# Seven products in place of eight for the last two slabs of the second mixer's input projection

## The chip, the cores and the metric

The kernel runs on one core of one Trainium2 chip, in fp32 throughout. The metric is the device time of one execution in microseconds (us), as the median of several runs. PE is TensorE (matmuls), PEld its weight loads, DVE VectorE, ACT ScalarE, POOL GpSimd, SP SyncE, which issues nearly all DMAs here. SBUF is the on-chip memory, PSUM the eight banks into which matmuls write. "L875" is line 875 of the kernel before.

## What is computed

Two layers over 256 tokens of width 1024, each a mixer (attention) and then a mixture of experts, with residual adds. The change lies in the input projection of the second layer's mixer:

```python
def _mixer_c(h, w_in, qn, kn, w_out):
    proj = jnp.einsum('bsd,de->bse', h, w_in)        # 1024 -> 1536 columns
    q, k, v = jnp.split(proj, C_SPLITS, axis=-1)     # 16 query heads, 4 key and value heads of 64
    q = _rmsnorm(q.reshape(b, S, C_HEADS, HEAD_DIM), qn)
    k = _rmsnorm(k.reshape(b, S, C_KV_HEADS, HEAD_DIM), kn)
    q = _apply_axial_rope(q, cr, sr, cc, sc)
    k = _apply_axial_rope(k, cr, sr, cc, sc)
    o = _dense_blocked_attention(q, k, v).reshape(b, S, C_QW)
    return jnp.einsum('bse,ed->bsd', o, w_out)
```

Behind it follow the output projection, the residual, the router and 32 experts, each a SwiGLU MLP of width 256, all of whose weights are read from HBM (96 MB per layer).

## The kernel before

**Weights.** All weights stream through slots of 1 MB in SBUF: 19 slots of `ring` (0 to 18), four of `shared`, one in `xT` and one in `heads` at the times when these are free. The units are numbered in the order of use: layer 0 has 9 slabs of the input projection (0 to 8), 4 output units and 96 expert units, layer 1 has slabs 109 to 114, output units 115 to 118 and expert units from 119 on. `place_units` fixes for each unit its slot and whose use it waits for; SP issues the loads in this order (L743, or L747 where several units go together), and waits in front of each until its slot is free (`s_used`, counted by PE). A load whose slot is not free holds back all behind it.

**Slabs.** A slab is 256 columns of the projection: 8 chunks of 128 rows by two halves of the tokens, 16 matmuls 128x128x256 into one PSUM bank (L875; `open_slab` at L850 for slab 0). The profile counts two records for each fp32 matmul of the source, so a slab is 32 records. `parts(s, 0, 1, 2, 3)` are its quarters. In layer 1, slab 0 holds the keys, slab 1 the values, slabs 2 to 5 four query heads each. Behind a slab of queries or keys, ACT copies it to `unturned` and squares it (L1316, L1317), DVE makes the inverse root (`norm`, L1673 to L1699) and the rotation (`rotate`, L1712 to L1729 or L1736), PE transposes it (`turn`, L957, L954) and ACT copies it to `heads` (L1380).

**Attention** goes by pairs of heads: `scores` on PE (L977), `maxima` on DVE (L1746), exponentials on ACT (L1394), `normalise` on DVE (L1773, L1776), `turn_prob` on PE (L994) with a copy on ACT (L1409), `prob_values` on PE (L1005) with a copy on ACT (L1413). Pairs 0 and 1 need slab 2, pairs 2 and 3 slab 3, pairs 4 and 5 slab 4, pairs 6 and 7 slab 5. `rows((cp, k))` is one piece of the output projection (L1017): quarter cp of the output, head pair k; it adds to a bank that already holds the residual (`residual(cp)`, ACT, L1432).

**Seven products.** Layer 0 treats six of its slabs in three pairs (`PAIRED`) by Strassen's scheme in Winograd's form. A pair of slabs is seen as a 2x2 block product (token halves by halves of the contraction, halves of the contraction by the two slabs): seven products of 4 matmuls, 8 records each (L891), instead of eight. It needs four sums of the input (`tokens`, L1616, once), four of the weights (`weights`, L1630, per pair, one of them written over a slab's weights), and five sums of products on DVE (`add_product`, L1638 to L1657) with three copies on ACT. Product order is 1, 5, 6, 7, 2, 3, 4. The slab named second is complete after product 3, the first after product 4. The sums lie in ring slots 15 to 17.

**Order.** One list per layer, `ORDER_0` and `ORDER_1`, is written out by hand. Each engine goes through the same list and issues its own part of each entry, and then works strictly in this order; waits are on semaphores. In layer 1, before:

```python
            + each("norm", 1) + each("rotate", 2) + parts(3, 0, 1, 2, 3) + parts(4, 0) + each("turn", 2) + parts(4, 1)
            + each("norm", 2) + attend(0) + parts(4, 2, 3) + each("residual", 0) + each("rotate", 3)
            + each("normalise", 0) + parts(5, 0) + each("norm", 3)
            + each("turn_prob", 0) + attend(1) + each("turn", 3) + parts(5, 1)
            + each("prob_values", 0) + each("normalise", 1) + parts(5, 2)
            + each("turn_prob", 1) + each("rotate", 4) + attend(2) + parts(5, 3) + each("residual", 1)
            + each("prob_values", 1) + each("normalise", 2) + rows((0, 0))
            + each("turn_prob", 2) + attend(3) + each("turn", 4) + rows((0, 1), (1, 0))
```

`norm` counts groups: group 0 is slab 0, groups 1 to 4 are slabs 2 to 5; `rotate` and `turn` count slabs.

## Time and profile before

| | us |
|---|---|
| median of 3 runs | 615.95 (615.41 to 616.2) |
| profiled execution | 618.22, span in the trace 616.1 |
| PE busy | 563.8 (92%) |
| DVE busy | 207.0 (34%) |
| ACT busy | 136.0 (22%) |
| HBM read | 231.60 MB, 378 GB/s over the span |

The span is the time from the first to the last event of the trace; the device time of the same execution is 2.1 us longer. Layer 1 begins at about 318 us in the trace, its experts at about 430 us. A busy share is a mean over stages with different limits: what counts is which wait ends last in the stage of the change. Tables by stage, timelines of single engines and the chain that ended last are read for that.

### The profile page before, as it was taken

How to read it: one execution, taken by the hardware profiler on the slowest of the kernel's cores; microseconds unless marked ns; L12 is line 12 of the kernel's file. 1: busy time of each engine (PE TensorE's matmuls, PEld its weight loads, DVE VectorE, ACT ScalarE, POOL GpSimd, SP SyncE). 2: the span in 40 equal slices, each digit the busy share in tenths (PEclk: the TensorE clock that was granted, in tenths of full speed). 3: DMA queues.
4: the chain of work that ended last, by engine and by line, in shares of the span. 5: the costliest groups of instructions: out<-in, count | busy, mean ns of one | idle time of the engine just before them, and what ended most of it. 6: DMA issues, size and time to landing. Idle time of an engine off the chain costs nothing.

```text
span 616.1 us, 9586 instructions
## 1 busy us (share of the span) xinstructions
PE 563.8 (92%) x3876; PEld 373.2 (61%) x3876; DVE 207.0 (34%) x631; ACT 136.0 (22%) x354; POOL 8.6 (1%) x25
## 2 busy tenths in 40 slices
PE   7999999998999949998999999999899996997997
PEld 6887877883555333555468876779355535434454
DVE  3778766153111101111035687416211111011101
ACT  2134547241001101001031366524100110110101
POOL 1100000000000000000011000000000000000000
PEclk8999999999999969999999999999999997999899
DMA  8992899789999999999999994539999999999996
GB/s 319 423 422 73 321 423 420 272 316 429 424 426 439 433 415 439 425 429 414 421 415 421 421 419 191 205 135 341 391 424 427 428 438 428 427 431 433 412 420 262
DMA packets 24229, 233.39 MB, mean 379 GB/s; under 512 B 2672, under 2 KB 3312, under 8 KB 6640
## 3 DMA queue, kind: packets, MB, share of 16 engines
q1 hardware_dynamic: 22448, 228.19, 88.8%
q10 hardware_dynamic: 1728, 4.47, 2.0%
q8 instruction: 36, 0.59, 0.4%
q14 instruction: 17, 0.14, 0.1%
HBM read 231.60 MB, written 1.05 MB: 378 GB/s over the span
## 4 chain that ended last, share of the span: by engine, by line
PE 58%; DMA 20%; issue 4%; ACT 3%; DVE 2%; DVEq 0%
DMA ring<-in_moe_w 20%; PE banks L1151 13%; PE banks L1017 8%; PE banks L1125 7%; PE banks L875 6%; PE banks L1221 6%; PE banks L1237 5%; PE banks L977 2%; PE banks L1005 1%; PE banks L994 1%; PE banks L1136 1%; PE banks L1028 1%; PE banks L1053 1%; PE banks L850 1%; PE banks L1094 1%
## 5 line engine op out<-in xcount | busy, mean ns | idle before, releaser
L1151 PE MATMUL banks<-ring,desk 128*32 128x512 f32 x736 | 86.4, 608 | 6.3 <-DMA ring<-in_moe_w 6.2
L1497 ACT ACTIVATE desk<-banks 128x256 f32<-128x256 f32 x16 | 6.1, 384 | 272.8 <-PE banks L1151 272.8
L1125 PE MATMUL banks<-desk,hT 128*128 128x128 f32 x384 | 49.9, 293 | 14.2 <-issue 14.2
L1017 PE MATMUL banks<-heads,ring 128*128 128x256 f32 x256 | 61.7, 386 | 0.1
L1125 PEld LDWEIGHTS banks<-desk,hT 128*128 128x128 f32 x384 | 49.4, 209 | 15.5 <-issue 15.0
L1151 PEld LDWEIGHTS banks<-ring,desk 128*32 128x32 f32 x736 | 22.8, 112 | 55.8 <-issue 50.8
L1017 PEld LDWEIGHTS banks<-heads,ring 128*128 128x128 f32 x256 | 46.4, 190 | 11.9 <-issue 6.2
L1221 PE MATMUL banks<-ring,desk 128*32 128x512 f32 x400 | 46.2, 595 | 8.1 <-ACT desk L1499 6.2
L1237 PE MATMUL banks<-desk 128*128 128x256 f32 x224 | 52.1, 386 | 0.0
L1237 PEld LDWEIGHTS banks<-desk 128*128 128x128 f32 x224 | 41.4, 190 | 16.8 <-issue 11.7
L875 PE MATMUL banks<-ring,hT 128*128 128x256 f32 x224 | 50.3, 381 | 0.0
L1913 DVE TENSOR_TENSOR desk<-banks,desk 128x256 f32<-128x256 f32 x16 | 6.8, 425 | 121.7 <-ACT desk L1497 121.7
L875 PEld LDWEIGHTS banks<-ring,hT 128*128 128x128 f32 x224 | 41.8, 190 | 6.4 <-issue 1.0
L1878 DVE TENSOR_TENSOR desk<-banks,gains_xT 128x512 f32<-128x512 f32 x24 | 16.6, 692 | 82.8 <-PE banks L1125 82.8
L1919 DVE COPY desk<-banks 128x512 f32<-128x512 f32 x14 | 9.7, 691 | 67.9 <-PE banks L1221 67.9
L1221 PEld LDWEIGHTS banks<-ring,desk 128*32 128x32 f32 x400 | 11.8, 109 | 32.7 <-issue 23.5
L891 PE MATMUL banks<-ring 128*128 128x256 f32 x96 | 22.9, 385 | 0.0
L891 PEld LDWEIGHTS banks<-ring 128*128 128x128 f32 x96 | 17.6, 190 | 3.9 <-issue 1.8
L850 PE MATMUL banks<-ring,hT 128*128 128x256 f32 x64 | 16.7, 423 | 2.0 <-DVE hT L1592 2.0
L1187 PE MATMUL banks<-small,desk 128*128 128x128 f32 x32 | 6.9, 297 | 12.4 <-DVE desk L1913 12.4
L977 PE MATMUL banks<-shared,heads 64*128 64x256 f32 x128 | 18.1, 402 | 0.1
L1151 PE MATMUL banks<-ring,heads 128*32 128x512 f32 x128 | 16.2, 601 | 1.9 <-DMA ring<-in_moe_w 1.9
(205 smaller groups left out, 654.0 us busy)
## 6 DMA issues: line engine op xcount, KB each, us to landing
ring<-in_moe_w SPq DMA_DIRECT2D x66, 1024.0 KB, 26.5
ring<-in_moe_w SPq DMA_DIRECT2D x16, 4096.0 KB, 26.8
ring<-in_moe_w SPq DMA_DIRECT2D x17, 2048.0 KB, 12.3
ring<-in_ab_w_in SPq DMA_DIRECT2D x8, 1024.0 KB, 17.0
shared<-in_moe_w SPq DMA_DIRECT2D x8, 1024.0 KB, 7.5
shared<-in_moe_w SPq DMA_DIRECT2D x2, 4096.0 KB, 30.9
shared<-in_moe_w SPq DMA_DIRECT2D x3, 2048.0 KB, 16.2
ring<-in_c_w_in SPq DMA_DIRECT2D x5, 1024.0 KB, 20.6
```

Source lines behind the costliest of these rows:

```text
L850: ins = pe.matmul(bank2(SLAB_BANK[layer][0], NT)[:, t, :], hT[:, c, t * P:(t + 1) * P], slab_weights(layer, 0)[:, c, :], start=(c == 0 and ...
L875: ins = pe.matmul(bank2(SLAB_BANK[layer][s], NT)[:, t, :], hT[:, c, t * P:(t + 1) * P], w[:, c, :], start=(c == 0 and t == 0), stop=(c == ...
L891: ins = pe.matmul(out, a[:, c, :], b[:, c, :], start=(start and c == 0), stop=(c == NC // 2 - 1), skip_group_check=True)
L977: ins = pe.matmul(bank2(r, NT)[:, t, :], heads[rows, i, t * P:(t + 1) * P], keysT[rows, kt, :], start=(t == 0), stop=True, skip_group_chec ...
L1017: ins = pe.matmul(bank2(Y[cp], 2)[:, c % 2, :], w[:, k % 2, c * P:(c + 1) * P], attT[:, k, :], start=False, stop=(k == PAIRS - 1 and c % 2 ...
L1125: ins = pe.matmul(bank(2 + half)[:, c * P:(c + 1) * P], tokens[:, t, half * HALF + c * P:half * HALF + (c + 1) * P], onehot_of(rd, to)[:, ...
L1151: ins = pe.matmul(bank(0)[j * SLOTS:(j + 1) * SLOTS, :], gathered_of(rd, place)[:, c, j * SLOTS:(j + 1) * SLOTS], w[:, j, :], start=(c == ...
L1187: pe.transpose(bank(4)[:, k * P:(k + 1) * P], hidden[:, k * P:(k + 1) * P], ident)
L1221: ins = pe.matmul(bank(2 + half)[j * SLOTS:(j + 1) * SLOTS, :], hiddenT[:, k, j * SLOTS:(j + 1) * SLOTS], w, start=(k == 0), stop=(k == 1))
L1237: ins = pe.matmul(bank2(Y[c // 2], 2)[:, c % 2, :], outputs[:, c * P:(c + 1) * P], scatter, start=False, stop=(c % 2 == 1), skip_group_che ...
L1878: V.tensor_tensor(gathered_of(rd, place)[:, 4 * h:4 * h + 4, :], bank2(2 + h, 4), gains[:, 2 * rd.layer + 1, 4 * h:4 * h + 4].unsqueeze(2) ...
L1919: V.tensor_copy(outputs[:, HALF:D], bank(3)).then_inc(sig.out_v, 1)
```

## The change

Slabs 5 and 4 of layer 1 become a fourth pair in `PAIRED` (first 5, second 4), with the banks 6 and 7 (slabs 4 and 5 exchange their banks) and half of bank 5, the bank of `turn`, for product 4. The sums of the tokens are made again from the second layer's input, in the same place. In `place_units` the slots 15 to 17 take no unit of layer 1 until both slabs of the pair are used; DVE waits in front of the first sums until the last units of layer 0 in these slots are used (`SUMS_FREE`). `ORDER_1` gets the token sums at its head, the weight sums behind the rotation of slab 0, the seven products in place of the eight quarters of slabs 4 and 5, and some entries change places: the norm of slab 4 goes behind product 4, `residual` 0 and 1 and the output rows (0,0) and (1,0) are moved. Helper functions get the layer or the pair as an argument. The core of the diff:

```diff
-PAIRED = ((3, 4), (5, 6), (8, 7))
+PAIRED = ((3, 4), (5, 6), (8, 7), (5, 4))
+IN_FIRST = 3
 SUMS_AT = 15
+SUM_SLOTS = 3
...
+        if layer:
+            last = first_unit(1, "in") + max(PAIRED[IN_FIRST])
+            left = [free[s] for s in range(SUMS_AT, SUMS_AT + SUM_SLOTS)]
+            for s in range(SUMS_AT, SUMS_AT + SUM_SLOTS):
+                free[s] = (last, last)
...
-        SLAB_BANK = [[6, 7, 2, 7, 6, 6, 7, 6, 7], [2, 3, 6, 7, 6, 7]]
+        SLAB_BANK = [[6, 7, 2, 7, 6, 6, 7, 6, 7], [2, 3, 6, 7, 7, 6]]
...
         ORDER_1 = (
-            each("sums", 0) + each("rstd", 0) + each("norm", 0) + each("rotate", 0) + parts(1, 0, 1, 2, 3)
+            each("tokens", 1) + each("sums", 0) + each("rstd", 0) + each("norm", 0) + each("rotate", 0)
+            + sums(3, 3, 1, 2, 4) + parts(1, 0, 1, 2, 3)
             + each("values", 1) + parts(2, 0, 1) + each("turn", 0) + parts(2, 2) + [("turn", 0, 1)] + parts(2, 3)
-            + each("norm", 1) + each("rotate", 2) + parts(3, 0, 1, 2, 3) + parts(4, 0) + each("turn", 2) + parts(4, 1)
-            + each("norm", 2) + attend(0) + parts(4, 2, 3) + each("residual", 0) + each("rotate", 3)
-            + each("normalise", 0) + parts(5, 0) + each("norm", 3)
-            + each("turn_prob", 0) + attend(1) + each("turn", 3) + parts(5, 1)
-            + each("prob_values", 0) + each("normalise", 1) + parts(5, 2)
-            + each("turn_prob", 1) + each("rotate", 4) + attend(2) + parts(5, 3) + each("residual", 1)
-            + each("prob_values", 1) + each("normalise", 2) + rows((0, 0))
-            + each("turn_prob", 2) + attend(3) + each("turn", 4) + rows((0, 1), (1, 0))
+            + each("norm", 1) + each("rotate", 2) + parts(3, 0, 1, 2, 3) + products(3, 1) + each("turn", 2) + products(3, 5)
+            + each("norm", 2) + attend(0) + products(3, 6) + each("rotate", 3) + products(3, 7)
+            + each("normalise", 0) + products(3, 2)
+            + each("turn_prob", 0) + attend(1) + each("turn", 3) + each("residual", 0) + products(3, 3)
+            + each("prob_values", 0) + each("normalise", 1) + products(3, 4) + each("norm", 3)
+            + each("turn_prob", 1) + each("residual", 1) + each("rotate", 4) + attend(2) + rows((0, 0))
+            + each("prob_values", 1) + each("normalise", 2) + rows((1, 0))
+            + each("turn_prob", 2) + attend(3) + each("turn", 4) + rows((0, 1))
...
-            return bank2(0, NT)[:, 1, :] if pair == len(PAIRED) - 1 else pair_banks(pair)[0][:, 1, :]
+            spare = {IN_FIRST - 1: 0, IN_FIRST: 5}
+            return bank2(spare[pair], NT)[:, 1, :] if pair in spare else pair_banks(pair)[0][:, 1, :]
...
                 if j == 1:
-                    if pair:
+                    if layer:
+                        slab_taken(pe, 1, 2)
+                    elif pair:
                         pe.wait_ge(s_tiles, 3 * pair - 1)
                     else:
                         slab_taken(pe, 0, 1)
-                    slab_arrived(0, first)
+                    slab_arrived(layer, first)
                     multiply(x[:, 0, :], hT[:, low_half, rows_0], wa[:, low_half, :], start=True).then_inc(s_prod, 1)
                 elif j == 5:
-                    if pair:
+                    if layer:
+                        slab_taken(pe, 1, 3)
+                    elif pair:
                         pe.wait_ge(s_tiles, 3 * pair)
                     else:
                         slab_taken(pe, 0, 0)
-                    pe.wait_ge(s_tsum, 1)
+                    pe.wait_ge(s_tsum, 4 * layer + 1)
                     pe.wait_ge(s_wsum, 4 * pair + 2)
                     multiply(y[:, 0, :], token_sum[:, 0, :, :], wb[:, low_half, :], start=True).then_inc(s_prod, 1)
...
                     pe.wait_ge(s_wsum, 4 * pair + 4)
                     pe.wait_ge(s_c11, pair + 1)
-                    if pair == len(PAIRED) - 1:
+                    if layer:
+                        pe.wait_ge(s_hT, turns_before(1, second))
+                    elif pair == IN_FIRST - 1:
                         pe.wait_ge(s_sc, NT * A_HEADS)
                     multiply(fourth_of(pair), hT[:, high_half, rows_1], t4, start=True).then_inc(s_used, 2)
...
+                    if layer and s == PAIRED[IN_FIRST][1]:
+                        pe.wait_ge(s_tiles, 3 * len(PAIRED))
...
-                if layer == 0 and cp == 0:
-                    act.wait_ge(s_tiles, 3 * len(PAIRED) - 1)
-                elif layer == 0 and cp == 1:
-                    act.wait_ge(s_c11, len(PAIRED))
+                if cp < 2 and cp == layer:
+                    act.wait_ge(s_tiles, 3 * (IN_FIRST + layer) - 1)
                 elif cp < 2:
-                    slab_taken(act, layer, max(s for s in range(SLABS[layer]) if SLAB_BANK[layer][s] == Y[cp]))
+                    act.wait_ge(s_c11, IN_FIRST + layer)
                 elif cp == 2:
...
-            def add_tokens():
+            def add_tokens(layer):
                 a11, a21 = hT[:, 0:NC // 2, 0:P], hT[:, 0:NC // 2, P:SEQ]
                 a12, a22 = hT[:, NC // 2:NC, 0:P], hT[:, NC // 2:NC, P:SEQ]
                 s1, s2, s3, s4 = [token_sum[:, i, :, :] for i in range(4)]
-                dve.wait_ge(s_h, 4)
+                dve.wait_ge(s_h, 4 * (layer + 1))
+                if layer:
+                    dve.wait_ge(s_used, SUMS_FREE)
                 for i, (out, a, b, op) in enumerate(((s1, a21, a22, ALU.add), (s2, s1, a11, ALU.subtract),
                                                      (s3, a11, a21, ALU.subtract), (s4, a12, s2, ALU.subtract))):
-                    after(dve, s_tsum, i)
+                    after(dve, s_tsum, 4 * layer + i)
                     V.tensor_tensor(out, a, b, op).then_inc(s_tsum, 1)
...
                 if i == 3:
                     for s in PAIRED[pair]:
-                        unit_arrived(dve, s)
-                    if pair >= 2:
+                        unit_arrived(dve, at + s)
+                    if pair >= IN_FIRST:
+                        dve.wait_ge(s_used, SUMS_FREE)
+                    elif pair >= 2:
                         pair_done(dve, pair - 2)
                 else:
                     dve.wait_ge(s_wsum, 4 * pair + (3, 1, 2, 4).index(i))
...
+            def buffer_turned(pair, s):
+
+                if pair >= IN_FIRST:
+                    dve.wait_ge(s_slab, norm_slabs_before(1, s) - 1)
+                elif SLAB_PLAN[0][s][0] in ("heads", "keys"):
                     dve.wait_ge(s_hT_ps, turns_before(*NORMED[norm_slabs_before(0, s) - 1]))
```

On ACT, `take_product` copies product 1 to `kept`, product 5 to `fifth` and product 2 to the first slab's tile, and squares each finished slab, as in layer 0.

## Rows read from the trace of the kernel before

**Rows 1.** The page's slices: 40 of 15.4 us; granted clock in tenths, GB/s moved.

```profile
...
PEclk8999999999999969999999999999999997999899
...
GB/s 319 423 422 73 321 423 420 272 316 429 424 426 439 433 415 439 425 429 414 421 415 421 421 419 191 205 135 341 391 424 427 428 438 428 427 431 433 412 420 262
...
```

**Rows 2.** Table by stage: busy us (instructions) by engine, granted clock, DMA share, GB/s.

```profile
...
375.00:388.00 13.00, 12.69 (x82) 8.36 (x80) 11.24 (x38) 7.91 (x27) 0.00 (x0) 1.00 0.24 81
435.00:607.00 172.00, 150.93 (x1171) 82.30 (x1168) 25.14 (x51) 12.91 (x32) 0.00 (x0) 0.96 1.00 427
512.00:514.00 2.00, 0.00 (x0) 0.00 (x0) 0.00 (x0) 0.00 (x0) 0.00 (x0) 1.00 1.11 455
514.00:515.00 1.00, 0.00 (x0) 0.00 (x0) 0.00 (x0) 0.00 (x0) 0.00 (x0) 0.50 0.84 360
...
```

**Rows 3.** Timeline of SyncE's DMA issues: start, us, line, operation.

```profile
...
304.16 7.43 SPq L743 DMA_DIRECT2D ring<-in_c_w_in  x4
...
431.30 3.35 SPq L743 DMA_DIRECT2D ring<-in_moe_w  x3
...
```

**Rows 4.** The chain that ended last, in order of time: start, us, what.

```profile
...
338.94 10.36 PE banks L875 x48
...
379.85 0.69 DVE negmax L1746
...
389.30 1.13 PE banks L1017 x4
...
```

**Rows 5.** Timeline of PE: start, us, line, tiles, records, [idle before it].

```profile
...
286.27 3.64 PE L1221 MATMUL banks<-ring,desk 128*32 128x512 f32 x32 [1.90 <-DMA ring<-in_moe_w]
...
371.85 1.13 PE L977 MATMUL banks<-shared,heads 64*128 64x256 f32 x8
...
383.41 0.66 PE L994 MATMUL banks<-small,shared 128*128 128x128 f32 x4 [0.26 <-DVE shared L1776]
...
515.87 6.16 PE L1125 MATMUL banks<-desk,hT 128*128 128x128 f32 x32 [5.12 <-issue]
...
```

**Rows 6.** Timeline of DVE in layer 1, columns the same.

```profile
...
325.91 0.16 DVE L1570 TENSOR_SCALAR mean<-banks 128x2 f32<-128x2 f32 x1 [2.78 <-PE banks L860]
...
333.26 1.80 DVE L1736 TENSOR_TENSOR desk<-desk 128x256 f32<-128x256 f32 x4
341.83 0.69 DVE L1673 TENSOR_REDUCE head_ss<-shared 128x8 f32<-128x512 f32 x1 [6.76 <-ACT shared L1317]
...
352.64 1.29 DVE L1746 TENSOR_REDUCE negmax<-banks 128x2 f32<-128x512 f32 x2 [0.47 <-PE banks L977]
...
357.50 0.68 DVE L1673 TENSOR_REDUCE head_ss<-shared 128x8 f32<-128x512 f32 x1
...
360.84 1.28 DVE L1746 TENSOR_REDUCE negmax<-banks 128x2 f32<-128x512 f32 x2
...
364.25 0.42 DVE L1712 TENSOR_TENSOR desk<-shared 128x256 f32<-128x256 f32 x1
...
367.15 1.29 DVE L1746 TENSOR_REDUCE negmax<-banks 128x2 f32<-128x512 f32 x2 [0.60 <-PE banks L977]
...
373.08 1.29 DVE L1746 TENSOR_REDUCE negmax<-banks 128x2 f32<-128x512 f32 x2 [2.43 <-PE banks L977]
...
```

**Rows 7.** The page's costliest groups: busy us, mean ns, idle before.

```profile
...
L875 PE MATMUL banks<-ring,hT 128*128 128x256 f32 x224 | 50.3, 381 | 0.0
...
L891 PE MATMUL banks<-ring 128*128 128x256 f32 x96 | 22.9, 385 | 0.0
...
```

**Rows 8.** Timeline of DVE in layer 0: sums of tokens, weights and products.

```profile
...
19.32 0.69 DVE L1616 TENSOR_TENSOR ring<-hT 128x512 f32<-128x512 f32 x1
...
28.40 5.00 DVE L1630 TENSOR_TENSOR ring<-ring 128x1024 f32<-128x1024 f32 x4
...
71.29 0.42 DVE L1638 TENSOR_TENSOR shared<-shared,banks 128x256 f32<-128x256 f32 x1 [0.46 <-PE banks L891]
...
```

**Rows 9.** The last four slab loads of layer 1, from issue to landing.

```profile
...
DMA to landing us min/median/max: 20.0/20.5/21.1
```

More of the change, by code:

```diff
@@ L154, in place_units @@
 def place_units():
-    last = max(PAIRED[-1])
+    last = max(PAIRED[IN_FIRST - 1])
     free = {s: (-1, None) if s < SUMS_AT else (last, last) for s in range(LOW)}
@@ L192, in place_units @@
             (high if s >= LOW else free)[s] = (seen, n)
-    return where
-WHERE = place_units()
+    return where, max(int(n) for n, _ in left) + 1
+WHERE, SUMS_FREE = place_units()
 def hybrid_moe_kernel(nc, xT_d, small_d, bias_d, rope_d, ab_in, ab_out, c_in, c_out, experts_d, out_d):
@@ L882, in product @@
                 first, second = PAIRED[pair]
+                layer = layer_of(pair)
                 x, y = pair_banks(pair)
-                wa, wb = slab_weights(0, first), slab_weights(0, second)
-                t2, t3, t4 = [weight_sums[:, pair % 2, i, :, :] for i in range(3)]
+                wa, wb = slab_weights(layer, first), slab_weights(layer, second)
+                t2, t3, t4 = [weight_sums[:, sums_region(pair), i, :, :] for i in range(3)]
                 low_half, high_half = slice(0, NC // 2), slice(NC // 2, NC)
@@ L923, in product @@
                     pe.wait_ge(s_v, pair + 1)
-                    pe.wait_ge(s_tsum, 4)
-                    slab_arrived(0, second)
+                    pe.wait_ge(s_tsum, 4 * layer + 4)
+                    slab_arrived(layer, second)
                     multiply(y[:, 0, :], token_sum[:, 3, :, :], wb[:, high_half, :]).then_inc(s_prod, 1)
@@ L1318, in slab, with room_for @@
                              ACT.Square).then_inc(s_sqh, 1)
[L1320 to L1322 removed]
+            def room_for(layer, s):
+                i = norm_slabs_before(layer, s)
                 act.wait_ge(s_slab, i - 1)
[L1324 removed]
+                if layer == 0:
+                    act.wait_ge(s_hT_ps, turns_before(*NORMED[i - 1]))
             def take_product(pair, j):
                 first, second = PAIRED[pair]
+                layer = layer_of(pair)
                 x, y = pair_banks(pair)
@@ L1336, in take_product @@
                     product_done(act, pair, 2)
-                    kind, _, col, _ = SLAB_PLAN[0][first]
+                    kind, _, col, _ = SLAB_PLAN[layer][first]
                     if kind == "values":
@@ L1342, in take_product @@
                     if kind != "shared2":
-                        room_for(first)
-                    A.activation(tile_of(first, 0), x[:, 0, :], ACT.Copy).then_inc(s_c11, 1)
+                        room_for(layer, first)
+                    A.activation(tile_of(pair, first, 0), x[:, 0, :], ACT.Copy).then_inc(s_c11, 1)
                 elif j in (3, 4):
@@ L1641, in add_product @@
                     dve.wait_ge(s_u, pair + 1)
-                    if pair and SLAB_PLAN[0][PAIRED[pair - 1][0]][0] == "values":
+                    if 0 < pair < IN_FIRST and SLAB_PLAN[0][PAIRED[pair - 1][0]][0] == "values":
                         dve.wait_ge(s_val, values_before(0, PAIRED[pair - 1][0]) + 1)
                     V.tensor_tensor(widened, kept, y[:, 1, :], ALU.add).then_inc(s_v, 1)
-                    buffer_turned(second)
+                    buffer_turned(pair, second)
                     dve.wait_ge(s_p5, pair + 1)
                     dve.wait_ge(s_v, pair + 1)
-                    V.tensor_tensor(tile_of(second, 1), widened, fifth, ALU.add).then_inc(s_tiles, 1)
+                    V.tensor_tensor(tile_of(pair, second, 1), widened, fifth, ALU.add).then_inc(s_tiles, 1)
                 elif j == 3:
@@ L1651, in add_product @@
                     dve.wait_ge(s_tiles, 3 * pair + 1)
-                    V.tensor_tensor(tile_of(second, 0), kept, y[:, 0, :], ALU.add).then_inc(s_tiles, 1)
+                    V.tensor_tensor(tile_of(pair, second, 0), kept, y[:, 0, :], ALU.add).then_inc(s_tiles, 1)
                 elif j == 4:
@@ L1965, in _ @@
                     elif what == "tokens":
-                        add_tokens()
+                        add_tokens(layer)
                     elif what == "weights":
```

41 lines of the change are left out of this document (21 added, 20 removed).

## The prediction

> **What bounds the kernel now.** I read the page's slices first. The two layers look alike: a mixer, then experts. In the experts the DMA engines move 410 to 440 GB/s without a break; in the second mixer they fall to 191, 205 and 135 GB/s [rows 1]. The table by stage says the same: from 435 us to 607 us the DMA share is 1.00, from 375 to 388 us it is 0.24, with TensorE (PE) busy for 12.69 of the 13 us [rows 2]. So the tail is bound by transfers, and the time at which it may begin is set by PE in the second mixer: the ring is full, and SyncE waits for slots. The load that ends the last standstill is the three expert units issued from 431.30 us [rows 3], when the first expert unit of layer 1 has been used. By my reading of the planner, units 0 to 143 are under way at that point both before and after, so whatever the mixer takes more or less reaches the end one for one.
>
> What bounds the mixer itself is told by the chain of waits. Up to 371.85 us it is PE's own work. Then it leaves PE: maxima of pair 3 on VectorE (DVE) at 373.08, maxima of pair 4 at 379.85, maxima of pair 5, ScalarE's (ACT) residual copy, and only at 389.30 PE again, with the row (2,0) [rows 4, 5, 6]. Between 373.08 and 389.30 lie 16.2 us of DVE and ACT work with no slack. Before it DVE has some: it waited 2.43 us for PE at 373.08 and 0.60 at 367.15 [rows 6]. This is where the change works.
>
> **The change part by part.** A source matmul is two records, one record 0.216 us (10.36 us for 48) [rows 4].
>
> Products for slabs: slabs 4 and 5 are 64 records, seven products of 8 are 56. Removed 13.8 us, added 12.1: PE is 1.7 us shorter. Product records of layer 0 have the duration of slab records (385 against 381 ns) [rows 7].
>
> Token sums: four DVE operations of 0.69 us, 0.73 apart [rows 8], 2.9 us. They stand where DVE waits 2.78 us for PE before 325.91. The rotation of slab 0 ends at 333.26 + 1.80 = 335.06, PE wants it at 336.2, so up to 1.1 us more would be hidden [rows 6]. Cost 0; without that cover 2.9.
>
> Weight sums: four of 1.22 us, 5.0 together [rows 8]; from 335.06 they end at 340.1, inside the 6.76 us in which DVE waits for slab 2 (until 341.83) [rows 6]. Cost 0. They wait for slabs 4 and 5: the issues of the last four slabs end at 311.6, landing takes 21.1 us at most, so 332.7 against 335.06 [rows 3, 9]. If slab 5 came late, slab 2's norm, queued behind, would wait; 1.7 us of that is free.
>
> Three ring slots kept until product 4: five expert loads (units 129 to 133) wait for it and issue near 366 us. DMA may pause for some 4 us before it, but the pause comes out of the standstill that starts at 375 us anyway [rows 2], since the next loads wait for the last slab's rotation. Cost 0, and nothing in the mixer needs them.
>
> "Fifth slab rotated in front of the third pair's maxima": rotation of slab 4 at 364.25, maxima 2 at 367.15 [rows 6]: it stood in front before, too. What moves is the norm of slab 4. Before, slab 4 was complete early and its norm ran at 357.50, between normalise 0 and maxima 1 (360.84: 3.34 us) [rows 6]. Now it is ready only after product 3, and the list puts norm and rotation behind product 4's sum. That is the step on which I place the forecast, so the queues in turn, from the end of slab 3 at 347.4:
>
> PE: product 1 to 349.2, turn 2 to 349.6, product 5 to 351.3, scores 0 to 352.4, products 6, 7, 2 to 357.6. DVE: maxima 0 at 352.64 as before. From there to the end of normalise 0 it needed 4.86 us (to 357.50) [rows 6]; inserted are the sum after product 6 (waits until 354.2, 0.4 of idle) and two after product 7, each 0.35 to 0.42 as in layer 0 [rows 8], 1.2 us. Normalise 0 ends at 359.1 and turn_prob 0 is over at 359.6 where PE could have been at 358.5: **1.1 us of the 1.7 are lost here**.
>
> PE on: scores 1 360.6, turn 3 361.1, product 3 362.9, values 0 363.9, product 4 365.6, turn_prob 1 366.5, scores 2 367.6, row (0,0), values 1, row (1,0) to 370.3. DVE: maxima 1, sum of product 3 (to 363.3), normalise 1 (to 364.8), sum of product 4 (waits, to 366.1), norm of slab 4 + 3.34 = 369.4, rotation + 2.2 = 371.6, **maxima 2 at 371.6, before 367.15** [rows 6]. PE has nothing left that it may do: turn_prob 2 needs normalise 2. Where DVE set the pace (pair 4), the second head's transposes began 3.56 us after the maxima (379.85 to 383.41), and they take 0.6 until the next scores, 4.15 in all [rows 4, 5]. Pair 2's so end at 375.75, and scores 3 start there, before at 371.85 [rows 5]: +3.9.
>
> Scale of the sum: the same durations put end to end give before's own third scores 0.5 us too early by the view, half of it taken up by the waits on DVE: +0.2, so I take +4.0 (rounded down). From scores 3 on the DVE chain of 16.2 us is the same in both, and it has no slack to give back. Row (1,0), pulled ahead, fills PE but is not on that chain. Mixer: **+4.0 us**.
>
> On the other queues: ACT gets three copies and two squares of 0.4 to 0.6 us instead of two slabs' copies and squares; its product 4 squares stand in front of turn_prob 1's copies, but product 4's sum (366.1) precedes those transposes' end anyway. Cost 0.
>
> Bounds: if the 1.1 us at turn_prob 0 is not lost (sums hidden), +2.9. If every sum costs 0.42 and each hand-over 0.1 more, +4.6. The profiled run took 618.22 (span 616.1 and 2.1 around it), the median is 615.95; the shift is added to both: 622.2 profiled, **620.0 as median**.
>
> **The rivals.** (a) *PE's idle time halves its clock.* In the gap of about 3.9 us ahead of turn_prob 2 PE does nothing. The trace shows a gap of 5.12 us before 515.87, in which the granted clock is 1.00 until 514 us and then falls to 0.50 (1.2 GHz); the 32 records behind it take 6.16 us [rows 2, 5]; the one of 1.90 before 286.27 left it high [rows 1, 5]. 3.9 lies between. If it falls, half a turn_prob (0.5) and scores 3 (1.06) are paid twice on the chain: +1.5, giving 621.5. For: nearer to 5.12 than to 1.9. Against: the clock was still 1.00 for over 3 us of that gap. The Trainium skill, "TensorE: Matmul & The Clock Gate", section "HAM oscillation — how this bites in real kernels", warns against such idle gaps in PE, each paid with a cold start; by it this case would be the likelier, by the rows it may just escape.
>
> (b) *PE's saving arrives: faster.* Place: turn_prob 2. If normalise 2 is ready when PE has done row (1,0), PE goes on 1.7 us early (0.7 with the loss at turn_prob 0), and the chain from scores 3 starts earlier by as much: 614.3 to 615.3. For this maxima 2 has to start by 367.8, so norm 3 by 362.2, before product 3 is even out (362.9). For it speaks only that PE is the busier engine in the mixer (12.69 of 13 us busy against DVE's 11.24 [rows 2]); against it the order of DVE's queue.
>
> (c) *The shift is partly absorbed behind the mixer*: the row at 389.30 had slack I don't see, or loads pace the rows. 617 to 618.5. Behind 389.30 the chain goes on with PE's own work and no wait up to the experts, so little speaks for it.
>
> (d) *The change does not do what it says*, the rotation being in front already: in itself 0, and contained in the forecast.
>
> **How the numbers follow.** Forecast (+2.9 to +4.6) 0.56, (a) 0.20, (b) 0.10, (c) 0.14, of which 0.08 within the bound. About 0.2% (1.2 us) is what a measurement of this kernel can tell from no change. Slower by more: 0.56 + 0.20 + 0.06 = 0.82; within 0.08; faster 0.10. The range reaches from 618.0 (upper part of (c)) to 622.0 (above (a) with 0.5 of spread) and leaves out (b) and the rest of (c).
>
> **What would show it.** Right: in the profile after, maxima 2 near 371.6 to 372, an idle time of PE of 3 to 4 us in front of turn_prob 2, scores 3 near 375.8, DVE without gaps from about 366 to 376, the row (2,0) near 393.3, and the load behind the first expert unit at 435.3. The sums of tokens and weights should lie in what were gaps, with turn 0 still at 336.2. Clock: 0.50 in 374 to 380 would be (a). Wrong: maxima 2 before 368; or maxima 2 late and the load of 431.3 not late; or a wait of the weight sums for slab 5, which would show as a late norm of slab 2 after 341.83.

## The result: 622.47 us, where 615.68 was measured before

Timed beside the kernel before, the changed kernel takes **622.47 us** (median of 6 runs, 621.93 to 624.28) against 615.68 us (614.81 to 616.2): ratio 1.0116, interval 1.0100 to 1.0131. It is slower by 6.8 us. The forecast was 620.0 us with a range from 618.0 to 622.0, so the direction is right and the size is not. The changed program was timed twice more, each time beside new runs of before, and was slower by 5.7 and 6.4 us there.

The page of the changed kernel, to set beside [rows 1]: the span, busy time of PE and DVE, granted clock in tenths of full speed and GB/s in 40 slices of 15.5 us.

```profile
span 620.2 us, 9596 instructions
...
PE 565.3 (91%) x3868; PEld 373.9 (60%) x3868; DVE 216.2 (35%) x644; ACT 136.2 (22%) x355; POOL 11.5 (2%) x25
...
PEclk9999999999999969999999997999999997999899
...
GB/s 325 423 422 59 388 420 424 268 314 435 424 425 444 415 435 433 427 431 412 417 418 420 422 296 192 203 93 377 352 430 426 438 428 428 434 424 431 416 421 262
```

The slices with little DMA in the second mixer now read 192, 203 and 93 GB/s where they read 191, 205 and 135. Slices of 15 us are coarse and lie differently against the two mixers; by how much the loads come later is told by their issue times below. The experts behind run at the same rate.

**A clock for the mixer.** Spans alone mislead here: in the profiled execution of before, layer 0 happens to be about 2 us longer than in most others (layer 1 begins at 318.46 us there, at 318.28 in e2 and at 315.8 to 316.8 in all others). So I count the mixer from its own start, the first slab's 32 records, to the issue of the three expert units behind which the tail begins. The start, in the timeline of PE of the kernel before, and then start and end in those of PE and of SP's queue of the changed kernel:

```profile
...
318.46 7.07 PE L850 MATMUL banks<-ring,hT 128*128 128x256 f32 x32
...
```

```profile
...
316.46 7.07 PE L866 MATMUL banks<-ring,hT 128*128 128x256 f32 x32
...
```

```profile
...
435.60 3.34 SPq L759 DMA_DIRECT2D ring<-in_moe_w  x3
...
```

That is 119.14 us, and before it was 431.30 [rows 3] less 318.46 = 112.84: the mixer is **6.30 us longer**. From that load to the end it is 184.6 us, before 184.8. The tail hands the shift on one for one. Times of the changed kernel called "aligned" below have 2.00 us added.

DVE in layer 1, to set beside [rows 6] (start, us, line, tiles, count, [idle before it, and what ended it]):

```profile
...
323.28 0.69 DVE L1643 TENSOR_TENSOR ring<-hT,ring 128x512 f32<-128x512 f32 x1
323.90 0.16 DVE L1595 TENSOR_SCALAR mean<-banks 128x2 f32<-128x2 f32 x1
...
333.02 5.00 DVE L1660 TENSOR_TENSOR ring<-ring 128x1024 f32<-128x1024 f32 x4
...
339.82 0.69 DVE L1705 TENSOR_REDUCE head_ss<-shared 128x8 f32<-128x512 f32 x1 [1.80 <-ACT shared L1342]
...
350.63 1.29 DVE L1778 TENSOR_REDUCE negmax<-banks 128x2 f32<-128x512 f32 x2 [0.47 <-PE banks L1002]
352.49 0.42 DVE L1668 TENSOR_TENSOR shared<-shared,banks 128x256 f32<-128x256 f32 x1 [0.57 <-PE banks L908]
...
355.03 0.41 DVE L1674 TENSOR_TENSOR shared<-shared,banks 128x256 f32<-128x256 f32 x1
355.58 0.42 DVE L1678 TENSOR_TENSOR shared<-shared 128x256 f32<-128x256 f32 x1
...
359.33 1.29 DVE L1778 TENSOR_REDUCE negmax<-banks 128x2 f32<-128x512 f32 x2 [1.88 <-PE banks L1002]
...
364.63 0.42 DVE L1687 TENSOR_TENSOR shared<-shared,banks 128x256 f32<-128x256 f32 x1 [1.17 <-PE banks L908]
364.96 0.68 DVE L1705 TENSOR_REDUCE head_ss<-shared 128x8 f32<-128x512 f32 x1
...
370.63 1.28 DVE L1778 TENSOR_REDUCE negmax<-banks 128x2 f32<-128x512 f32 x2
...
377.41 1.29 DVE L1778 TENSOR_REDUCE negmax<-banks 128x2 f32<-128x512 f32 x2 [3.28 <-PE banks L1002]
...
```

L1778 is the maxima. Those of pair 2 start at 370.63, aligned 372.63, where before had 367.15. They stand behind norm and rotation of slab 4 (from 364.96), and the norm stands behind product 4's sum (364.63), though the slab it needs was complete after product 3. Those of pair 3 start at 377.41, aligned 379.41, where before had 373.08: +6.33, the whole of the mixer's loss. The maxima of pair 4 follow 6.76 us later (384.17), in before 6.77.

PE around the place, beside [rows 5]:

```profile
...
356.88 1.29 PE L1019 MATMUL banks<-small,shared 128*128 128x128 f32 x8 [0.97 <-DVE shared L1808]
...
368.53 1.13 PE L1042 MATMUL banks<-heads,ring 128*128 128x256 f32 x4
373.27 2.03 PE L1019 MATMUL banks<-small,shared 128*128 128x128 f32 x8 [3.60 <-DVE shared L1808]
375.23 2.08 PE L1002 MATMUL banks<-shared,heads 64*128 64x256 f32 x8
...
```

PE idles 3.60 us in front of turn_prob 2 (L1019), and the scores behind it (L1002) take 2.08 us, where the third scores of before took 1.13 [rows 5]. The table by stage says why (stretch, length, busy time of PE, PEld, DVE, ACT and POOL, granted clock, DMA share, GB/s):

```profile
...
370.00:372.00 2.00, 0.00 (x0) 0.00 (x0) 1.89 (x3) 0.66 (x3) 0.00 (x0) 1.00 0.97 369
372.00:373.00 1.00, 0.00 (x0) 0.00 (x0) 0.57 (x3) 1.00 (x5) 0.00 (x0) 0.64 1.00 418
373.00:374.00 1.00, 0.73 (x4) 0.71 (x4) 0.87 (x4) 0.55 (x3) 0.00 (x0) 0.50 1.08 451
374.00:376.00 2.00, 2.00 (x10) 1.40 (x10) 0.13 (x1) 1.20 (x2) 0.00 (x0) 0.50 0.97 410
...
378.00:379.00 1.00, 1.00 (x4) 0.82 (x3) 0.70 (x2) 0.87 (x4) 0.00 (x0) 0.50 0.87 369
379.00:380.00 1.00, 1.00 (x7) 0.58 (x7) 0.78 (x3) 1.00 (x7) 0.00 (x0) 0.95 0.20 82
...
```

The granted clock falls to 0.50 (1.2 GHz) within the gap and stays there until about 379 us: rival (a) has come true.

### The profile page after: what moved, and what is told of

It is laid out like the page before. It is cut to its first block, busy times and chain, and to the rows that moved or that the text cites. A ratio compares the mean times of both kernels' runs of the same rounds, so it can differ in the third digit from the quotient of the medians.

```text
span 620.2 us, 9596 instructions
## 1 busy us (share of the span) xinstructions
PE 565.3 (91%) x3868; PEld 373.9 (60%) x3868; DVE 216.2 (35%) x644; ACT 136.2 (22%) x355; POOL 11.5 (2%) x25
## 3 DMA queue, kind: packets, MB, share of 16 engines
HBM read 231.60 MB, written 1.05 MB: 375 GB/s over the span
## 4 chain that ended last, share of the span: by engine, by line
PE 58%; DMA 19%; issue 4%; DVE 4%; ACT 3%; DVEq 0%
DMA ring<-in_moe_w 19%; PE banks L1176 13%; PE banks L1042 8%; PE banks L1150 7%; PE banks L1246 6%; PE banks L1262 6%; PE banks L891 3%; PE banks L1002 2%; PE banks L1019 2%; PE banks L908 1%; PE banks L1030 1%; PE banks L1161 1%; PE banks L1053 1%; PE banks L1078 1%; PE banks L866 1%
## 5 line engine op out<-in xcount | busy, mean ns | idle before, releaser
L891 PE MATMUL banks<-ring,hT 128*128 128x256 f32 x160 | 35.4, 380 | 0.0
L891 PEld LDWEIGHTS banks<-ring,hT 128*128 128x128 f32 x160 | 30.1, 190 | 3.9
L908 PE MATMUL banks<-ring 128*128 128x256 f32 x128 | 30.4, 384 | 0.0
L908 PEld LDWEIGHTS banks<-ring 128*128 128x128 f32 x128 | 23.4, 190 | 4.9 <-issue 2.1
L908 PE MATMUL banks<-ring,hT 128*128 128x256 f32 x96 | 22.7, 383 | 0.1
L908 PEld LDWEIGHTS banks<-ring,hT 128*128 128x128 f32 x96 | 17.7, 190 | 3.7 <-issue 1.5
L1660 DVE TENSOR_TENSOR ring<-ring 128x1024 f32<-128x1024 f32 x16 | 19.6, 1223 | 0.3
L1002 PE MATMUL banks<-shared,heads 64*128 64x256 f32 x128 | 19.1, 419 | 0.1
```

The source lines that it names most:

```text
L891: ins = pe.matmul(bank2(SLAB_BANK[layer][s], NT)[:, t, :], hT[:, c, t * P:(t + 1) * P], w[:, c, :], start=(c == 0 and t == 0), stop=(c == ...
L908: ins = pe.matmul(out, a[:, c, :], b[:, c, :], start=(start and c == 0), stop=(c == NC // 2 - 1), skip_group_check=True)
L1002: ins = pe.matmul(bank2(r, NT)[:, t, :], heads[rows, i, t * P:(t + 1) * P], keysT[rows, kt, :], start=(t == 0), stop=True, skip_group_chec ...
L1660: V.tensor_tensor(out, a, b, ALU.subtract).then_inc(s_wsum, 1)
```

## The experiments

All are read by the mixer's length, taken as above. Medians and ratios are those of several runs beside before; the other columns are of one profiled execution. PE busy is over the mixer's interval.

| kernel | median us | ratio (interval) | mixer us | against before | PE busy us |
|---|---|---|---|---|---|
| before | 615.68 to 616.13 | | 112.84 | | 112.39 |
| changed | 622.47 | 1.0116 (1.0100 to 1.0131) | 119.14 | +6.30 | 114.09 |
| e7, the same again | 621.67 | 1.0091 (1.0077 to 1.0105) | 118.81 | +5.97 | |
| e10, the same again | 622.10 | 1.0112 (1.0095 to 1.0129) | 118.86 | +6.02 | |
| e1, PE kept busy | 621.72 | 1.0092 (1.0067 to 1.0117) | 117.76 | +4.92 | |
| e9, the same again | 621.07 | 1.0083 (1.0069 to 1.0097) | 117.76 | +4.92 | 114.67 |
| e11, half as busy | 622.03 | 1.0101 (1.0085 to 1.0116) | 119.17 | +6.33 | |
| e2, norm late in before | 617.38 | 1.0018 (1.0008 to 1.0027) | 114.17 | +1.33 | |
| e3, sums without products | 615.78 | 0.9993 (0.9982 to 1.0005) | 112.85 | +0.01 | |
| e6, two entries moved | 618.90 | 1.0044 (1.0031 to 1.0058) | 115.81 | +2.97 | |
| e4, products, other order | 613.98 | 0.9969 (0.9958 to 0.9981) | 110.79 | -2.05 | 110.16 |
| e8, the same again | 613.95 | 0.9962 (0.9948 to 0.9976) | 110.79 | -2.05 | |
| e5, before, other order | 614.51 | 0.9978 (0.9968 to 0.9988) | 111.50 | -1.34 | 111.50 |

The tail from the load to the end is 184.5 to 184.9 us in all of them.

**PE kept busy in the gap (e1, e9).** In `turn_prob` of the changed kernel, 14 matmuls whose results nobody reads fill most of the gap (0.49 us of it is left):

```diff
+                if layer and i == 2:
+                    pe.wait_ge(s_pT, HEADS + 2 * i)
+                    warm_up(2, ident, 14)
```

> The changed kernel, with 14 matmuls of the identity by itself (128x128x128 each, 0.22 us each, some 3.1 us in all, into a bank that is overwritten next) in front of turn_prob of pair 2 in the second mixer, where PE stands idle for 3.60 us. Their results are not used. Theory 'queue and clock': of the 6.3 us by which the maxima of pair 3 come late against the kernel before, 1.4 us are the halved clock behind the gap (the transposes of turn_prob 2 take 2.03 us in place of 1.04, scores 3 take 2.08 in place of 1.13). With PE busy in the gap the granted clock stays at 1.00, maxima 3 begin about 5.4 us behind maxima 2 in place of 6.78, and the time falls by 1.4 us: about +5.4 us against the kernel before (621.1). Rival 'the chain does not care': PE's slow stretch is covered by DVE's and ACT's work, then the clock stays up and the time stays within 0.3 us of the changed kernel.

> The changed kernel with 14 identity matmuls in PE's gap, once more, now beside the changed kernel on the same chip, since the first run was told by few executions. Theory 'the halved clock costs on the chain': 1.0 to 1.4 us below the changed kernel. Rival 'the clock costs nothing in the end': equal to it within 0.3 us.

The timeline of PE in e1, and three stretches of its table:

```profile
...
369.41 3.29 PE L1056 MATMUL banks<-small 128*128 128x128 f32 x28
373.19 0.66 PE L1022 MATMUL banks<-small,shared 128*128 128x128 f32 x4 [0.49 <-DVE shared L1811]
374.10 0.66 PE L1022 MATMUL banks<-small,shared 128*128 128x128 f32 x4 [0.26 <-DVE shared L1811]
374.69 1.13 PE L1002 MATMUL banks<-shared,heads 64*128 64x256 f32 x8
...
```

```profile
...
372.00:373.00 1.00, 0.70 (x7) 0.51 (x5) 0.65 (x3) 1.00 (x6) 0.00 (x0) 1.00 1.04 442
373.00:374.00 1.00, 0.66 (x4) 0.42 (x4) 0.87 (x4) 0.59 (x4) 0.00 (x0) 1.00 0.99 418
374.00:376.00 2.00, 1.90 (x14) 1.36 (x15) 0.13 (x2) 1.08 (x2) 0.00 (x0) 1.00 1.01 426
...
```

With work in the gap the clock stays at 1.00 (2.4 GHz), the scores take 1.13 us again, and from the maxima of pair 2 to those of pair 3 it is 5.38 us (370.54 to 375.92) instead of 6.78. The mixer is 1.38 us shorter, in both traces. In device time it is 1.0 us (621.07 for e9 against 622.10 for e10, measured side by side); the ratios' intervals (1.0069 to 1.0097, 1.0095 to 1.0129) touch, so the trace carries this more firmly than the medians. What is left at full clock, +4.92, is not the clock's; e2, e3, e6 and e4 below show how much of it is the order's.

**The changed kernel again (e7, e10).** The same program, measured beside the others on their chip.

> The changed kernel itself, beside the others on the same chip: 6.3 to 6.8 us above the kernel before. It shows whether the halved clock behind the gap is there in another profile (the transposes of turn_prob 2 at 2.0 us, scores 3 at 2.1 us).

> The changed kernel, for the comparison with the kernel above and the one below: 5.7 to 6.8 us above the kernel before, the halved clock behind the gap in front of turn_prob 2 again.

Its excess over before scatters (5.7, 6.4, 6.8 us; e7 came out under the 6.3 to 6.8 that I expected), and the traces give a reason for some of it: the moment at which the clock falls is not the same. In e10, PE and the table by stage:

```profile
...
372.61 0.66 PE L1019 MATMUL banks<-small,shared 128*128 128x128 f32 x4 [3.62 <-DVE shared L1808]
373.52 0.79 PE L1019 MATMUL banks<-small,shared 128*128 128x128 f32 x4 [0.26 <-DVE shared L1808]
374.24 2.08 PE L1002 MATMUL banks<-shared,heads 64*128 64x256 f32 x8
...
```

```profile
...
372.00:374.00 2.00, 1.13 (x8) 0.84 (x8) 1.34 (x5) 1.49 (x6) 0.00 (x0) 0.98 1.05 438
374.00:376.00 2.00, 2.00 (x10) 1.19 (x8) 0.00 (x0) 0.60 (x1) 0.00 (x0) 0.50 0.97 410
376.00:378.00 2.00, 2.00 (x10) 1.57 (x8) 1.29 (x2) 0.86 (x4) 0.00 (x0) 0.67 1.07 451
...
```

The idle time is the same (3.62 us), but the clock falls only just before 374, when the transposes are nearly done: they cost 0.13 more than at full clock instead of 0.45, the scores 0.95 in both. So the same gap costs 1.10 us here (118.86 less 117.76) and 1.38 in the first trace. e7 is like e10: the two heads' transposes take 0.65 and 0.77 us, not the 2.0 in all that I expected, and the scores 2.08.

**Half as much filler (e11).** The edit of e1 with 6 matmuls instead of 14.

> The changed kernel with 6 identity matmuls (1.3 us) at the start of the same gap of 3.6 us, so that PE is idle for about 2.3 us in front of turn_prob 2. In the traces so far stalls of 1.46 and 1.90 us left the granted clock at 1.00, those of 3.60 us let it fall. If the fall takes a gap of nearly the full length, the clock stays up and the time is that of the 14 matmuls; if any idle time over some 2 us is enough, it falls to 0.50 and the time is that of the changed kernel.

```profile
...
369.43 1.50 PE L1056 MATMUL banks<-small 128*128 128x128 f32 x12
373.21 0.66 PE L1022 MATMUL banks<-small,shared 128*128 128x128 f32 x4 [2.28 <-DVE shared L1811]
374.12 1.12 PE L1022 MATMUL banks<-small,shared 128*128 128x128 f32 x4 [0.25 <-DVE shared L1811]
375.16 2.08 PE L1002 MATMUL banks<-shared,heads 64*128 64x256 f32 x8
...
```

```profile
...
373.00:374.00 1.00, 0.66 (x4) 0.42 (x4) 0.87 (x4) 0.59 (x4) 0.00 (x0) 0.95 0.99 418
374.00:376.00 2.00, 1.88 (x8) 1.47 (x10) 0.06 (x1) 1.10 (x2) 0.00 (x0) 0.50 1.02 430
...
```

The filler leaves 2.28 us of idle time, and the clock falls all the same, just before 374 us, when PE is at work again; the second head's transposes take 1.12 us instead of 0.66, the scores 2.08. The mixer takes 119.17 us, as in the first trace of the changed kernel (119.14), and 0.3 more than in e10 beside it. A filler that covers the gap in part buys nothing here.

That a gap of this length is enough doesn't hang on the filler. In layer 0 of e6, PE had worked without a break for 14 us (257.71 to 272.14), and then stood idle for 2.56 us:

```profile
...
274.70 5.34 PE L1176 MATMUL banks<-ring,desk 128*32 128x512 f32 x32 [2.56 <-DMA ring<-in_moe_w]
...
```

The granted clock reads 1.00 up to 275 us, 0.55 over 275 to 276 and 0.50 over 276 to 278, and the 32 records take 5.34 us. After an idle time of 2.38 us at the same place in e11 they take 5.34 too; after 1.97 us in e8, 3.64 us at a clock of 1.00.

**The norm of slab 4 late, without any product (e2).** In before's list:

```diff
-            + each("normalise", 0) + parts(5, 0) + each("norm", 3)
+            + each("normalise", 0) + parts(5, 0)
...
-            + each("prob_values", 0) + each("normalise", 1) + parts(5, 2)
+            + each("prob_values", 0) + each("normalise", 1) + parts(5, 2) + each("norm", 3)
```

> The kernel before (plain slabs, no sums, no products) with one entry moved: the norm of slab 4 stands where the changed kernel has it, behind normalise 1 in place of behind normalise 0. Theory 'order of the DVE queue': norm and rotation of slab 4 (5.5 us) now stand together in front of the maxima of pair 2. Norm of slab 4 starts near 364.2 in place of 357.5, maxima 2 near 369.5 in place of 367.15, turn_prob 2 waits, and the mixer ends later by about 1.2 us (617.0 against 615.7). That is only a part of the changed kernel's delay, since here the norm can start 2.7 us earlier than behind product 4. Rival 'it is the sums and products themselves, not their order': no change within 0.3 us.

PE at turn_prob 2, in the kernel before and in e2:

```profile
...
370.88 1.04 PE L994 MATMUL banks<-small,shared 128*128 128x128 f32 x8
...
```

```profile
...
371.50 0.65 PE L994 MATMUL banks<-small,shared 128*128 128x128 f32 x4 [0.65 <-DVE shared L1776]
...
```

The maxima of pair 2 start 1.9 us later (50.58 us after the mixer's start instead of 48.69) and PE now waits 0.65 us for `normalise` in front of turn_prob 2, where before shows no wait. The mixer grows by 1.33 us and the median by 1.25. So the move of the norm alone, with every matmul as it was, makes the kernel slower, through the queue of DVE.

**The sums without the products (e3).** The changed kernel's slots, token sums and weight sums, with before's slabs, banks and order of slabs behind them; sum 1 goes to another region, so that slab 4's weights stay whole, and PE waits for all eight sums in front of slab 4.

```diff
+                    if layer and s == 4:
+                        pe.wait_ge(s_wsum, 4 * len(PAIRED))
+                        pe.wait_ge(s_tsum, 8)
```

> The changed kernel's sums without its products: token sums, weight sums and the three ring slots kept for them as in the changed kernel, but slabs 4 and 5 as eight quarters in the order of the kernel before, on the banks of before. The sums are not used. (One weight sum goes to the sums' own place, not over slab 4's weights; PE waits in front of slab 4 for sums that have long been made.) Theory 'queue and clock': the sums lie in idle time of DVE, the slots in a standstill of the loads, so the time is that of the kernel before within 0.3 us (615.7). Rival 'the sums or the slots cost': 0.5 to 3 us more, seen as a late turn of slab 0 or a late load behind the first expert unit.

The mixer takes 112.85 us against 112.84, and the ratio's interval holds 1. Eight DVE operations of 7.9 us in all, three slots held back and the wait for slabs 4 and 5 cost nothing: they lie in idle time.

**Two entries moved (e6).** In the changed kernel, the norm of slab 4 goes in front of product 4, as early as its data allows, and its rotation behind the maxima of pair 2. The second goes beyond the kernel before, where the rotation stood in front of these maxima too.

```diff
-            + each("prob_values", 0) + each("normalise", 1) + products(3, 4) + each("norm", 3)
-            + each("turn_prob", 1) + each("residual", 1) + each("rotate", 4) + attend(2) + rows((0, 0))
+            + each("prob_values", 0) + each("normalise", 1) + each("norm", 3) + products(3, 4)
+            + each("turn_prob", 1) + each("residual", 1) + attend(2) + each("rotate", 4) + rows((0, 0))
```

> The changed kernel with two entries moved in DVE's queue and nothing else: the norm of slab 4 in front of product 4's sum (it needs only product 3's), the rotation of slab 4 behind the maxima of pair 2. By the sum of durations maxima 2 start 3.0 us earlier, the idle time of PE in front of turn_prob 2 is split into 1.8 us before prob_values 1 and 0.5 us before turn_prob 2, and the mixer is 1.5 us shorter. Theory 'queue and clock': with no long gap left the granted clock stays at 1.00 too, another 1.4 us: 2.9 us less than the changed kernel, 619.5. Rival 'total DVE work, not the order, sets the delay': within 0.3 us of the changed kernel but for the clock, 621.1.

Timelines of PE, of DVE and of ACT:

```profile
...
369.26 1.08 PE L1030 MATMUL banks<-shared 128*64 128x256 f32 x8 [1.46 <-ACT shared L1436]
371.70 1.40 PE L1019 MATMUL banks<-small,shared 128*128 128x128 f32 x8 [0.30 <-DVE shared L1808]
...
```

```profile
...
367.11 0.41 DVE L1687 TENSOR_TENSOR shared<-shared,banks 128x256 f32<-128x256 f32 x1
367.44 1.28 DVE L1778 TENSOR_REDUCE negmax<-banks 128x2 f32<-128x512 f32 x2
...
```

```profile
...
367.61 0.63 ACT L1392 ACTIVATE shared<-shared 128x512 f32<-128x512 f32 x1 [3.60 <-issue]
368.14 1.06 ACT L1436 ACTIVATE shared<-banks 128x512 f32<-128x512 f32 x2
...
```

The maxima of pair 2 start at 367.44 instead of 370.63 (3.4 us earlier, counted from the mixer's start), the gap of 3.60 us is gone (0.30), the clock stays at 1.00 over the mixer, and the mixer is 3.33 us shorter than in the changed kernel; the medians measured together differ by 2.8 us (618.90 and 621.67), where 2.9 was expected. More than half of the loss, the clock's part included, hung on the place of these two entries in the list: 1.95 us of the 4.92 that are left at full clock, and the 1.38 of the clock. The rest, 2.97 us, stays, and a part of it shows as a new wait: `prob_values` 1 stalls 1.46 us for ACT's copy of turn_prob 1 (L1436). ACT works in its order too: in front of this copy stands the square of slab 5 (L1392), for which ACT stands idle 3.60 us until DVE has made product 4's sum (L1687, at 367.11), and that sum now stands behind the norm. The next longest waits of PE are 0.97 us in front of turn_prob 0 and 0.91 in front of turn_prob 4.

**Other orders (e4, e8 with the products; e5 without).** The whole list from slab 2 on is written anew, by adding up durations from these timelines for each engine's queue. The place of the change in e4:

```diff
...
-            + each("turn_prob", 0) + attend(1) + each("turn", 3) + each("residual", 0) + products(3, 3)
-            + each("prob_values", 0) + each("normalise", 1) + products(3, 4) + each("norm", 3)
-            + each("turn_prob", 1) + each("residual", 1) + each("rotate", 4) + attend(2) + rows((0, 0))
-            + each("prob_values", 1) + each("normalise", 2) + rows((1, 0))
+            + products(3, 2) + each("normalise", 1) + products(3, 3) + each("turn", 3) + each("residual", 0)
+            + each("prob_values", 0) + each("norm", 3) + each("turn_prob", 1) + each("residual", 1)
+            + each("scores", 2) + each("maxima", 2) + products(3, 4) + each("rotate", 4) + each("exponentials", 2)
+            + rows((0, 0)) + each("prob_values", 1) + each("normalise", 2) + rows((1, 0)) + each("maxima", 3)
...
```

> The changed kernel with nothing but its list ORDER_1 rearranged: scores of a pair ahead of the turn_prob of the pair before it (pairs 1, 3, 4, 5), product 6 behind scores 0's pair of entries on DVE, the norm of slab 4 directly behind the sum of product 3 and normalise 1, maxima 2 next, and only then product 4's sum and the rotation of slab 4; norm of slab 5 behind maxima 4. Theory 'queue and clock': with no entry on DVE standing in front of one that PE waits for, maxima 2 come within 1 us of the kernel before, no gap of PE is over 1 us, the clock stays up, and PE's 1.7 us are gained: 2.2 us less than the kernel before by the sum of durations, 613.5; with 0.5 us of hand-overs not counted 614.0. Rival 'the products make DVE the bound whatever the order': at least 2 us above the kernel before (617.7 or more), with DVE busy without a gap from 352 to 385 us.

> The reordered changed kernel once more, on the same chip as the reordered kernel before: 2.2 us below the kernel before as in its first run (ratio 0.9965), and 0.9 us below the reordered kernel before if the seven products are worth something by themselves; equal to it within 0.3 us if only the list is.

> The kernel before (plain slabs, no sums, no products) with its list ORDER_1 rearranged by the same method as the reordered changed kernel: entries of one kind keep their order, nothing is added or left out. By the sum of durations PE's idle time in the mixer falls from 1.4 to 0 us and the mixer is 1.3 us shorter: 614.8 against 616.1. Theory 'queue and clock': the list alone is worth 1.3 us, the seven products under a good list another 0.9 us. Rival 'the whole gain of the reordered kernel is its list': this kernel comes out at 614.0, as the reordered changed kernel does.

The only wait of PE of e4 between 345 and 395 us, and its maxima of pair 2:

```profile
...
382.36 1.16 PE L981 MATMUL banks<-small,desk 128*128 128x128 f32 x8 [0.49 <-DVE desk L1763]
...
```

```profile
...
364.32 1.28 DVE L1780 TENSOR_REDUCE negmax<-banks 128x2 f32<-128x512 f32 x2
...
```

The maxima of pair 2 start at 364.32, counted from the mixer's start 6.4 us earlier than in the changed kernel, since they stand in front of product 4's sum and the rotation. **This kernel beats both**: 613.98 and 613.95 us, ratios 0.9969 and 0.9962, 8 us below the changed kernel with the same work (7.7 us where both were measured together, e8 and e7). The same treatment of before's list gives 614.51 (e5), where PE is busy for all of the mixer's 111.50 us. So most of e4's gain over before is the order's, -1.34 of -2.05 us. Only 0.45 us of it was idle time of PE (112.84 less 112.39), not the 1.4 of my expectation; the other 0.89 is busy time that the same 655 records lose in the new order, most of it in the output rows (31.34 us for their 128 records before, 30.69 in e5). What the seven products themselves bring is the rest: 0.71 us by the mixer's length, 0.56 by the medians measured together (613.95 against 614.51; the two intervals overlap, 0.9948 to 0.9976 and 0.9968 to 0.9988), out of 1.7 us of removed matmuls. The two lists are not the same, so this compares the best order found for either. PE's busy time differs by 1.34 us (111.50 less 110.16): slabs and products together take 34.42 us where the slabs took 36.24, 1.82 less, and 0.23 comes back in the output rows and 0.15 in turn_prob. Of the 1.34 us, 0.63 comes back as waiting.

## Why the prediction was right in direction and short in size

**Right: where and why.** The place (DVE's queue between product 4's sum and maxima 2), the releaser (turn_prob 2 waiting for normalise 2), the gap (forecast 3 to 4 us, 3.60 measured) and the way to the end (one for one through the full ring) are all in the trace. e2 shows the cause by moving one entry in the kernel before, e6 by moving two in the changed kernel; e6 also shows that these two are not all of it (2.97 us stay). That the gap fell into my 3 to 4 us is in part luck: behind scores 2 PE still had three pieces to do, which take 3.2 us (366.46 to 369.66), and my sum had 2.7 for them, so the gap of "about 3.9 us" should have read about 3.4.

**Right: the terms set to nothing.** The token sums end at 323.97, and the mean behind them starts at 323.90, aligned 325.90, where before had 325.91: the 2.78 us cover them. The weight sums run from 333.02 and leave 1.80 us of waiting in front of slab 2's norm, forecast 1.7, and that norm starts at 341.82 aligned, before 341.83. DMA does pause before the held slots come free: the share is 0.22 between 362 and 365 us of the changed kernel's trace. e3 shows all of it together at +0.01.

**Right: the 16.2 us chain.** From the maxima of pair 3 on nothing is given back: the shift is +6.33 there and +6.30 at the load. Rival (c), absorption behind the mixer, is out. So is (b), for this order: its condition was maxima 2 by 367.8, and they came at 372.6. e4 meets it (366.2 aligned), and there the saving arrives, 0.6 to 0.7 us of it. The mechanism of (b) exists, and the list decides whether it acts.

**Wrong: the term "scale of the sum".** To the 3.9 us for scores 3 I added 0.1 for what lies between operations (my own test of the sum had shown 0.5 us too little, of which I took 0.2 and then rounded down); at full clock it is 4.92 (e1, e9), so the term is short by 0.9. The aligned timeline shows where it was lost, as the difference to my own times. Maxima 0 are exact (352.63 against 352.64). The end of normalise 0 is 0.36 late (359.46 against 359.1): product 6's sum starts after 0.57 us of idle time where I had 0.4, and the second sum behind product 7 starts 0.55 us after the first, where I had 0.35. Turn_prob 0 and scores 1 add 0.2, values 0 and product 4 another 0.25 (1.14 and 1.81 us for 1.0 and 1.7), norm and rotation 0.17 (5.67 us instead of 5.5). Sum: **1.0 us**, at maxima 2 (372.63 against 371.6). From there to scores 3 I had 4.15 us, and at full clock it is 4.14 (370.61 to 374.75 in e9). No term was wrong by much; but nearly all came out 0.03 to 0.2 us short, in one direction, on a path where every one counts. The upper bound had this case in it (+4.6, each hand-over 0.1 more) and was itself 0.3 too low.

**Wrong: the chance of rival (a).** I gave 0.20 to a fall of the clock and priced it at 1.5 us; it fell in all three traces of the changed program, and cost 1.38, 1.10 and 1.05 us by the mixer's length. The price was 0.1 to 0.45 us too high, which is near enough; the chance was too low. I had argued from the gap of 5.12 us in before, in which the clock still read 1.00 more than 3 us after the work had stopped [rows 2, 5]. The traces here say what I did not consider: that the fall comes late doesn't save the work behind the gap. In e7, e10 and e11 it came 0.7 to 1.3 us after PE had resumed, and hit the scores. The Trainium skill, "TensorE: Matmul & The Clock Gate", section "HAM oscillation — how this bites in real kernels", had warned of such gaps and of the cold start that each is paid with; three traces of the changed kernel with 3.60 to 3.62 us of idle time agree, and behind the gap of 1.46 us in e6 the clock stayed at 1.00.

**Together.** +3.9 (path, as forecast) + 1.0 (its hand-overs) + 1.4 (clock) = +6.3 us, which is the mixer's +6.30. The forecast had the first and 0.1 of the second. The range failed because its upper end took (a) on top of a central value that was itself 1 us low: with both, 615.95 + 6.3 = 622.3. Measured from the 615.68 us of the kernel before beside it, the sum gives 622.0, and 0.5 us of the measured 622.47 lie outside the mixer's account.

**Open.** The medians' excess (6.8, 5.7, 6.4 us) scatters more than the mixer does in the traces (6.30, 5.97, 6.02); 0.3 us of it is the moment of the clock's fall, the rest wasn't followed. Of the 2.97 us that stay in e6 the waits are known, but no run takes them away one by one; e4 shows only that another order of the whole list removes them. Why the same output rows take 0.65 us less of PE in e5's order isn't settled either.

## What to carry to other kernels

When a block of data is finished later, look for the first operation in an in-order queue that must now wait for it, and at what stands behind that operation: here a saving of 1.7 us on the busiest engine ended as a loss of 6.3 us, and 3.3 of these hung on the maxima, which needed nothing of it, standing behind the norm and the rotation. Move such entries together with the change (e4) before the saving is judged; here the order was worth more than the products that it carries (1.3 us against 0.7). An early place has its price in the other queues: in e6 it held back ACT's copy and PE with it by 1.46 us. And on a path that runs through three engines, take each hand-over from the row that shows this very hand-over, and add to a TensorE gap like those here (2.28 to 3.62 us) the slow clock behind it.

## What was unexpected of the hardware

- The same idle time of PE (3.60 and 3.62 us) was answered differently in two executions of one program: the granted clock fell at about 372.3 us (0.64 over 372 to 373), inside the gap, and was back soon after 379 (0.95 over 379 to 380); or it fell at 373.9 (0.98 over 372 to 374), 1.3 us after work had resumed, and was back at about 377.3 (0.67 over 376 to 378).
- 2.28 us of idle time behind 1.50 us of filler (e11) were enough for a fall, and so were 2.38 (e11) and 2.56 us (e6) in layer 0 behind unbroken work; 0.49 us (e1), 1.46 (e6), 1.90 [rows 5] and 1.97 us (e8) were not.
- The fall can come after work has resumed: 0.4 us after in layer 0 of e6 (resumed at 274.70, 0.55 over 275 to 276), 1.3 us after in e10.
- At 1.2 GHz the eight score records take 2.08 us instead of 1.13, the eight transposes behind the gap 2.03 instead of 1.58 (0.66 + 0.66 and the wait of 0.26 for DVE between them): the wait hides a part of the slow clock.
